# Convolution stage of a two-layer encoder: diagonals loaded, gate from PSUM, two staggered tap lanes, norm in token rows

## The reference

```
h = x @ w_in + b_in                      # 1024 -> 2048
a, gate = jnp.split(h, 2, axis=-1)
h = a * jax.nn.sigmoid(gate)
h = depthwise causal convolution of h, 31 taps per channel, + b_dw
h = jax.nn.silu(layer_norm(h, ln_g, ln_b))
mix = h @ w_out + b_out
x = layer_norm(DEEPNORM_ALPHA * x + mix, ln1_g, ln1_b)      # norm 0
```

## Time and profile before

| | value |
|---|---|
| median of three runs | 1872.43 us |
| the profiled execution's own time | 1870.53 us |
| its span | 1868.7 us |
| PE, DVE, ACT, POOL busy over the span | 97%, 69%, 50%, 15% |
| PE, DVE, ACT, POOL busy in 0 to 150 us | 128.7, 112.6, 93.0, 74.7 us |
| mean granted TensorE clock | 0.996 |
| bytes read from device memory | 316.95 MB |

### The profile page before, as it was taken

One profiled execution on the slowest core, in us unless ns is written; L12 is line 12 of the kernel. 1 busy time (PEld: TensorE's weight loads), 2 busy tenths in 40 slices (PEclk: granted clock), 3 DMA queues, 4 the chain that ended last, 5 costly groups with the idle time before them and its releaser, 6 DMA issues.

```text
span 1868.7 us, 31371 instructions
## 1 busy us (share of the span) xinstructions
PE 1816.6 (97%) x12212; PEld 1652.7 (88%) x12212; DVE 1285.7 (69%) x2400; ACT 926.7 (50%) x1593; POOL 272.5 (15%) x145
## 2 busy tenths in 40 slices
PE   7989999999999999999999999999999999999998
PEld 7669999999999888888777899999999988888886
DVE  5974893888965666666665559668888556666665
ACT  6754544544444544555534454445444454445553
POOL 7800746000000000000002228430000000000000
PEclk9999999999999999999999999999999999999999
DMA  7325555545556666667722356555555566666662
GB/s 251 113 71 164 153 161 169 157 159 159 158 171 205 193 194 195 195 203 255 258 93 68 117 154 182 169 159 158 159 159 159 181 204 194 194 195 193 214 216 100
DMA packets 87843, 320.05 MB, mean 171 GB/s; under 512 B 9872, under 2 KB 10384, under 8 KB 87568
## 3 DMA queue, kind: packets, MB, share of 16 engines
q1 hardware_dynamic: 84672, 307.42, 53.2%
q10 hardware_dynamic: 3024, 10.62, 1.6%
HBM read 316.95 MB, written 1.05 MB: 170 GB/s over the span
## 4 chain that ended last, share of the span: by engine, by line
PE 89%; DVE 6%; ACT 2%; DMA 1%; issue 1%; POOL 0%; SPq 0%; ACTq 0%; DVEq 0%
PE work L480 42%; PE y L528 38%; PE y L761 3%; PE y L508 2%; DVE y L1440 2%; PE work L636 1%; PE y L734 1%; DMA raw<-v 1%; DVE low L409 1%; PE y L583 1%; DMA raw<-mla_in 0%; ACT high L805 0%; DVE big L1252 0%; PE work L577 0%; DVE big L1423 0%
## 5 line engine op out<-in xcount | busy, mean ns | idle before, releaser
L805 ACT ACTIVATE high<-raw 128x1024 fp32r<-128x1024 f32 x473 | 497.8, 1054 | 476.8 <-PE work L480 430.3
L480 PE MATMUL work<-xT_high,high 128*128 128x256 f32 x2368 | 679.0, 287 | 14.8 <-POOL low L409 10.1
L480 PE MATMUL work<-xT_low,high 128*128 128x256 f32 x2368 | 671.3, 283 | 0.0
L480 PE MATMUL work<-xT_high,low 128*128 128x256 f32 x2368 | 671.1, 283 | 0.0
L409 DVE TENSOR_TENSOR low<-raw,high 128x1024 fp32r<-128x1024 f32 x384 | 469.4, 1224 | 249.2 <-ACT high L805 248.1
L480 PEld LDWEIGHTS work<-xT_high,high 128*128 128x128 f32 x2368 | 455.6, 192 | 17.3 <-POOL low L409 10.3
L480 PEld LDWEIGHTS work<-xT_low,high 128*128 128x128 f32 x2368 | 455.8, 192 | 0.0
L480 PEld LDWEIGHTS work<-xT_high,low 128*128 128x128 f32 x2368 | 455.4, 192 | 0.0
L409 POOL TENSOR_TENSOR low<-raw,high 128x1024 fp32r<-128x1024 f32 x89 | 220.8, 2489 | 249.9 <-ACT high L805 249.7
L1054 ACT ACTIVATE xT_high<-big 128x256 fp32r<-128x256 f32 x256 | 105.4, 416 | 285.3 <-PE y L528 285.1
L528 PE MATMUL y<-high,xT_high 128*128 128x512 f32 x696 | 216.9, 392 | 6.5 <-DVE xT_low L1468 5.2
(11 more groups left out here) (183 smaller groups left out, 1523.8 us busy)
## 6 DMA issues: line engine op xcount, KB each, us to landing
raw<-u SPq DMA_DIRECT2D x256, 512.0 KB, 3.5
raw<-v SPq DMA_DIRECT2D x256, 512.0 KB, 3.5
raw<-wq SPq DMA_DIRECT2D x32, 512.0 KB, 3.5
raw<-conv_in SPq DMA_DIRECT2D x16, 512.0 KB, 4.7
aux<-ln_par ACTq DMA_DIRECT2D x9, 512.0 KB, 5.8
raw<-conv_out SPq DMA_DIRECT2D x8, 512.0 KB, 3.6
raw<-mla_out SPq DMA_DIRECT2D x8, 512.0 KB, 3.7
raw<-mla_in SPq DMA_DIRECT2D x6, 512.0 KB, 4.5
```

Source lines behind the costliest of these rows:

```text
L480: mm = nc.tensor.matmul(out_, w[:, cols], m[:, k, :], start=(k == 0 and n == 0), stop=(k == KD - 1 and n == 2))
L805: A(high_at(c), raw[:, slot, :], ACT.Copy).then_inc(high_made, 1)
```

## The change

Part by part:

- **Start.** `x_cols` is loaded and split in four parts instead of two, and block 0 in two halves.
- **Gate.** ACT empties only the gate half. DVE's `glu` reads the value straight from PSUM with the bias (one instruction, PSUM and SBUF inputs). `conv_in` uses four banks instead of three.
- **Diagonals.** They come from device memory as a new input `diag` (4.06 MB, eight loads, issued by ACT beside blocks 4 to 12) instead of being made by ACT.
- **Taps of DVE.** Chunks 0 and 2 run in lane 0, chunks 1 and 3 in lane 1; lane 0 starts 12 taps ahead; chunk 4 is shared, 22 taps in lane 0 and 9 in lane 1, and one addition joins them. The later `glu`s stand between taps.
- **Norm.** PE transposes the chunks into token rows (in PSUM), some of them within the diagonals' matmuls. DVE takes BN statistics along rows, scales rows, PE transposes back group by group (two chunks of one token half), ACT applies SiLU in place in PSUM.
- **High and low of blocks 17 to 27.** POOL stops after block 16 and goes to the taps of chunk 7; afterwards it makes 18, 19, 21, 22, 25, 27, and DVE makes 17, 20, 23, 24, 26. ACT makes high 20 and 21 between the two halves' SiLU and high 22 to 27 after them. `scale_x(1)` and all four lows of 24 to 27 come ahead of norm 0.

```diff
@@ gpsimd
-            low_stage(0, FIRST["conv_out"] + 2 * RING)
+            pool.wait_ge(first_high, 1)
+            nc.gpsimd.tensor_tensor(low[:, 0, left], raw[:, 0, left], high[:, 0, left].bitcast(F32),
+                                    ALU.subtract).then_inc(first_low, 1)
...
+            low_stage(1, FIRST["conv_out"] + 1)
...
+            for c in OUT_LOWS_POOL:
+                make_low(pool, nc.gpsimd, c)
@@ tensor
+                elif name == "conv_in":
+                    out_ = work[:, c % BANKS, 0:T]
+                    if c >= BANKS:
+                        chunk, gate = divmod(c - BANKS, 2)
+                        pe.wait_ge(emptied if gate else glu_ok, chunk + 1)
...
             for c, k in enumerate(PE_CHUNKS):
                 pe.wait_ge(glu_ok, k + 1)
+                pe.wait_ge(diag_in[c], 16 * DIAG_LOADS)
                 for w in range(TAPS):
-                    pe.wait_ge(diag_ok, c * TAPS + w + 1)
...
+                    if c == 1 and w == ROWS_AT:
+                        pe.wait_ge(emptied, KD)
+                        pe.wait_ge(glu_ok, KD)
+                        pe.wait_ge(conv_done, SHARED)
+                        for n in range(SHARED):
+                            rows = to_rows(n)
+                        rows.then_inc(rows_mm, 1)
+                        pe.wait_ge(pe_conv_ok, 1)
+                        to_rows(PE_CHUNKS[0])
                 mm.then_inc(pe_conv, 1)
+            pe.wait_ge(conv_done, SHARED + 1)
+            to_rows(SHARED).then_inc(rows_mm, 1)
+            pe.wait_ge(pool_conv, 1)
+            to_rows(POOL_CHUNK)
+            pe.wait_ge(pe_conv_ok, 2)
+            to_rows(PE_CHUNKS[1]).then_inc(rows_mm, 1)
 
             def wait_conv(c):
+                n = c - FIRST["conv_out"]
                 wait_low(c)
-                wait_xT(PARTS + c - FIRST["conv_out"] + 1)
+                if n % PER_GROUP == 0:
+                    wait_xT(X_PARTS + n // PER_GROUP + 1)
+                if n == 2:
+                    to_columns(0, 1)
+                elif n in (4, 5):
+                    to_columns(1, n - 4)
+            to_columns(0, 0)
+            combine_tail(FIRST["conv_out"], 0, wait_conv, True, wait_conv_half)
@@ scalar
-                for n in range(DIAGONALS * t, DIAGONALS * (t + 1)):
-                    diagonal(n)
...
+            def silu(h, g):
+                act.wait_ge(cols_mm, GROUPS * h + g + 1)
+                for k in range(PER_GROUP * g, PER_GROUP * (g + 1)):
+                    chunk = group_bank(h, g)[:, k % PER_GROUP, :]
+                    ins = A(chunk, chunk, ACT.Silu,
...
+                A(xT_high[:, ks, h * P:(h + 1) * P], group_bank(h, g), ACT.Copy).then_inc(xT_hi_ok, 1)
+            for g in range(GROUPS):
+                silu(0, g)
+            make_high(rounded[0])
+            make_high(rounded[0])
+            for g in range(GROUPS):
+                silu(1, g)
             highs_to(FIRST["wq0"] + LEAD["wq0"] - 1)
@@ vector
             def glu(k):
-                dve.wait_ge(emptied, 2 * k + 2)
-                V.tensor_tensor(padded[:, k, PAD:PAD + T], value[:, k, :], value_gate[:, k, :],
-                                ALU.mult).then_inc(glu_ok, 1)
+                dve.wait_ge(emptied, k + 1)
+                V.scalar_tensor_tensor(padded[:, k, PAD:PAD + T], work[:, 2 * k % BANKS, 0:T],
+                                       conv_p[:, C_BIN + k:C_BIN + k + 1], value_gate[:, k, :],
+                                       ALU.add, ALU.mult).then_inc(glu_ok, 1)
...
+            for g in range(GROUPS):
+                conv_low(0, g)
+            make_low(dve, V, FIRST["conv_out"] + 4)
+            for g in range(GROUPS):
+                conv_low(1, g)
+            make_low(dve, V, FIRST["conv_out"] + 7)
...
             scale_x(0)
-            low_stage(FIRST["wq0"], FIRST["wq0"] + 2)
+            scale_x(1)
+            make_low(dve, V, FIRST["wq0"])
+            make_low(dve, V, FIRST["wq0"] + 2)
```

More of the change, by code:

```diff
@@ L533, in combine_block, with combine_second_half @@
                 return mm
-            def combine_second_half(part, norm, blocks, turn_after):
+            def combine_second_half(part, norm, blocks, turn_after, wait_block=None):
                 for n in blocks:
+                    if wait_block is not None:
+                        wait_block(n)
                     mm = part(n, (1,), (0,))
@@ L553, in combine_tail @@
                 mm.then_inc(y_half, 1)
-                combine_second_half(part, norm, range(TAIL), TURN_AFTER)
+                combine_second_half(part, norm, range(TAIL), TURN_AFTER, wait_half)
             def turn_half(n, h):
@@ L858, in _ @@
+            left, right = slice(0, D // 2), slice(D // 2, D)
+            round_x(0)
+            act.wait_ge(first_landed, 16)
+            A(high[:, 0, left], raw[:, 0, left], ACT.Copy).then_inc(first_high, 1)
+            round_x(1)
+            act.wait_ge(landed[0], 16)
+            A(high[:, 0, right], raw[:, 0, right], ACT.Copy).then_inc(high_made, 1)
+            rounded[0] = 1
+            for part in range(2, X_PARTS):
+                round_x(part)
+            highs_to(RING - 1)
             act.wait_ge(conv_par_in, 16)
@@ L859, in _, with load_diagonals @@
             act.wait_ge(consts, 4)
-            def diagonal(n):
-                c, w = n // TAPS, n % TAPS
-                at = C_TAPS + PE_CHUNKS[c] * TAPS + w
-                A(diagonals[:, c, w, :], ident[:], ACT.Identity,
-                  scale=conv_p[:, at:at + 1]).then_inc(diag_ok, 1)
+            def load_diagonals(n):
+                c, part = divmod(n, DIAG_LOADS)
+                edges = [(part + i) * TAPS // DIAG_LOADS * P for i in range(2)]
+                act.dma_start(diagonals[:, c, edges[0]:edges[1]],
+                              diag[:, c, edges[0]:edges[1]]).then_inc(diag_in[c], 16)
@@ new lines, in _ @@
+            glu(0)
+            for _ in range(AHEAD):
+                next_tap(0)
+                dve.wait_ge(v_step, count[0])
+            glu(1)
+            while done[0] < lengths[0] or done[1] < lengths[1]:
+                for lane in (1, 0):
+                    if done[lane] < lengths[lane]:
+                        next_tap(lane)
+                    else:
+                        dve.wait_ge(v_step, count[0])
+            dve.wait_ge(v_step, count[0])
+            V.tensor_tensor(conv[:, SHARED, :], conv[:, SHARED, :], total_of(0, 2),
+                            ALU.add).then_inc(conv_done, 1)
@@ new lines, in measure_rows @@
+            def measure_rows(h, g):
+                col = 24 * h + 6 * g
+                return V.bn_stats(row_stats[:, col:col + 6], row_group(h, g))
+            dve.wait_ge(x_in, 16 * HALVES)
+            dve.wait_ge(ln_in[0], 16 * LN_ROWS[0])
+            for g in range(GROUPS):
+                if g != 1:
+                    dve.wait_ge(rows_mm, max(g, 1))
+                for h in range(HALVES):
+                    last = measure_rows(h, g)
+                if g == 1:
+                    make_low(dve, V, FIRST["conv_out"] + 1)
@@ L1472, in _ @@
-            dve.wait_ge(x_in, 16 * HALVES)
-            dve.wait_ge(ln_in[0], 16 * LN_ROWS[0])
+            step(V.reciprocal(row_stats[:, 56:58], row_stats[:, 54:56]))
+            for h in range(HALVES):
+                for g in (0, 2, 3):
+                    rows, n = (work[:, 2 * h, :], PART) if g == 0 else (row_group(h, g), PER_GROUP)
+                    cols = slice(PER_GROUP * g * P, (PER_GROUP * g + n) * P)
+                    last = V.tensor_scalar(rows_n[:, h, cols], rows,
+                                           row_stats[:, 48 + 2 * h:49 + 2 * h], row_stats[:, 56 + h:57 + h],
+                                           ALU.subtract, ALU.mult)
+                    if g != 2:
+                        last.then_inc(norm_ok, 1)
```

285 lines of the change are left out of this document (152 added, 133 removed).

## The result

The changed kernel is slower: 1876.05 us, median of 20 runs (1869.32 to 1879.29), against 1871.18 us for the kernel before, timed beside it (20 runs, 1869.39 to 1874.66). The ratio is 1.0022, 95% interval 1.0014 to 1.0030. The forecast was 3.5 us less; it came out 4.9 us more. The profiled execution took 1875.27 us (span 1873.5) against 1870.53, so it shows the difference nearly whole.

The account below looks back on a forecast made before the run. PE was taken as the bound from the leading query blocks on, so E's change counts one for one: 133.73 to 130.2, hence 1872.43 - 3.5 = 1868.9 us; own range 1867 to 1871, wider range 1862.5 to 1873.5.

Parts of the forecast that it names:

- E: End of the first layer's conv_out, where PE starts the leading query blocks: 130.2 us, 3.5 less than 133.73.
- late chain: Behind conv_out's start, later blocks' highs and lows pass ACT, POOL and DVE late; norm 0 follows, PE waits 2.8 us.
- S: Time at which the token rows are complete ahead of the norm: 86.9 us, ended by PE, not DVE.
- Start: First conv_in blocks: block 0 begins near 7 instead of 9.86, block 1 at 13.25 instead of about 15.0.
- s: Delay of conv_in blocks by the diagonals' 4.06 MB of loads: 1.0 us, bounds 0 and 4.
- Rival 3: Diagonals' loads starve the weight ring; s could be 8 and goes into E in full: 1875.9 us, chance 0.11.
- Taps of DVE: DVE's first tap after glu 0 at 16.7, twelve alone at 0.52, the rest at 0.392: end 83.2 instead of 95.0.
- Additions of POOL: Chunk 7's taps: products start at 60, 29 additions at 0.694 and a last one, ending at 82.2.
- Low 17: DVE makes this conv_out block's low within the 3.7 us it has to spare before the rows are complete.
- Norm: From complete rows to conv_out: statistics to reciprocal 1.9 us, six scalings 3.1, low half 0.4; conv_out starts at 92.3.
- The turn: PE at norm 0 after conv_out's first halves: wait 2.8 us, transposes 0.8, last six right blocks 4.1.
- Load of block 26: Weight load that waits for low 23 ahead of norm 0: 3.6 us, landing at 115.9.

Follow-up runs that it names:

- e12: Changed kernel with only DVE's queue ahead of norm 0 shortened (x scaled earlier, low 26 and high 27 after the first half's norm); 1871.73 us, ratio 1.0002.
- e5: Changed kernel with the old start: input in two parts, block 0 of conv_in whole, diagonals still loaded; 1873.64 us, ratio 1.0013.
- e1: Changed kernel loading two diagonals in place of 62 and using them for every tap, so taps of chunks 5 and 6 are not computed; 1878.26 us.
- e2: Changed kernel with the diagonals made by ACT again, three per block, without their loads; 1877.37 us, ratio 1.0027.
- e6: Changed kernel with both the divided start and the diagonals' loads undone (ACT makes the diagonals); 1875.49 us, ratio 1.0024.
- e4: Changed kernel with the same diagonal bytes spread over more blocks, x and the norm's rows loaded behind them; 1875.77 us, ratio 1.0023.
- e10: e8 with a shorter DVE queue ahead of norm 0 (x scaled earlier, low 26 after the first half's norm); 1862.43 us, ratio 0.9952.
- e8: e6 with the lows of conv_out blocks 17 to 20 and highs of 19 to 21 made earlier; 1871.06 us, ratio 1.0001.
- e7: Kernel before with the divided start alone (input in four parts, block 0 in two halves); 1871.98 us, ratio 1.0006.
- e11: Changed kernel with both the early lows of conv_out and the shorter queue ahead of norm 0; 1861.43 us, ratio 0.9947.

## Why the prediction was wrong

The forecast was E = 130.2 for the leading blocks; 138.86 was measured. The late chain of the prediction held in its kind: PE waits for POOL's low 21 and 22 (0.20 and 4.14 us; also 1.60 for DVE's low 20, which it did not name), DVE for high 26, norm 0 is late, PE idles ahead of L617, the clock is at its lower level when `conv_out` starts (twelve matmuls in 5.31 us, forecast 5.1). It priced `conv_out` to E at 37.9 us, and 39.5 were measured. The step that failed is what stands ahead: S, the time at which the rows are complete, and the start of `conv_out`, forecast at 86.9 and 92.3, measured at 92.5 and 99.40. A gain of 16.4 us was expected there to pay for 13 behind, and there were 9.3. Of the 8.7 us by which E was missed, 7.1 lie ahead of `conv_out` and 1.6 behind its start. The items below are read from the one profile of the changed kernel. No run brought `conv_out` to before 97.36, and the same front in e12 was 2 us faster, so their sizes are good to some 2 us.

- **Start.** Block 1 at 14.24, forecast 13.25: its load, behind seven transfers, was issued at 4.03 and landed at 10.69 (chain, 6.64). In the kernel before it stands behind four and was issued at 2.63. "The bytes ahead of block 1 are the same" was true and not enough; there are three more issues ahead of it, 0.4 to 0.5 us each.
- **s.** Forecast 1.0. Fifteen blocks after 14.24 would have ended at 57.4; PE went on to the diagonals at 63.47, so s was 6.0; 1.6 of these are block 15 at the lower clock, which the term had not. In e12 the same front gives 61.08, in e5, with the bytes but the old start, 58.82. Rival 3 described this and gave 1875.9, next to the time measured. But e1, e2 and e6 took the bytes away, e4 spread them, and the time stayed. Its number was right by luck; its mechanism was not the loss. The waits of ACT for blocks (20.9 us, 12.5 in e12, 3.3 in the kernel before) say that the ring of three covered less than s = 1.0 assumed: the share of 0.91 of the earlier trace rows left little. The Trainium skill ("DMA: Bandwidth & Descriptors", "Issuing engines are not separate DMA queues"), by which the two streams take from the same 16 DMA engines, had been cited and not turned into a price.
- **Taps of DVE.** Forecast to end at 83.2; the last addition ended at 88.2. First tap 18.51 instead of 17.1 (1.4); twelve taps alone took 7.1 instead of 6.25, their pitch is 0.59, not 0.52 (0.85); two `glu`s waited 1.7 for late blocks; the rest took 1.0 more. The room between DVE's taps and the complete rows was there all the same (88.2 to 92.5), but only because PE was late too; in e5, with PE on time, it was 1.0 us (87.6 to 88.6).
- **Additions of POOL.** Forecast to end at 82.2; they ended at 89.5, since ACT's products began at 67.28 and not at 60, behind a block of `conv_out` that landed at 66.3. So POOL's first low behind them fell onto DVE's low 17 (in e5, where the additions end at 86.4, it was the second).
- **Low 17.** Priced inside the 3.7 us of room at its own 1.2. It took 3.40: POOL's low ran from 89.45 to 91.80, and DVE's ended 1.1 after it. In e5, with PE early, it took 3.19. What this costs is seen in e4 against e12: the rows are complete at 89.8 and 90.1 and the taps end at 88.7 and 88.4, but the low takes 3.39 in e4 and 1.21 in e12, and `conv_out` starts at 99.60 and 97.36. The prediction had the Trainium skill's rule on the port ("SBUF — State Buffer", "Who interferes with whom") and used it for low 23, where it came true (2.53), but not here. DVE's last statistics, behind low 17, begin at 92.81, just when the rows are complete at 92.5. These are two tracks of equal length. In e1, e2, e4 and e5 PE's is shorter (rows complete at 90.0, 89.2, 89.8 and 88.6), but DVE's isn't (last statistics at 93.5, 91.8, 93.3 and 92.0), and `conv_out` moved by 1.1 us at most.
- **Norm.** From the rows to `conv_out` 6.9 us, forecast 5.4; of that DVE's low has 0.4, and the statistics to the reciprocal took 2.7 instead of 1.9 (four pieces of 256 were left, not two).
- **The turn.** PE waited 2.95 (forecast 2.8), but the transposes took 1.97 (forecast 0.8), because the granted clock fell after the wait (0.72 from 130 to 134), and the six right blocks behind them 4.6 (forecast 4.1). The lower clock was reckoned at the start of `conv_out` and not here.
- **Load of block 26.** 4.94 us, forecast 3.6.
- **"Moving `scale_x(1)` and two lows ahead of norm 0 saves nothing."** Right, but the reverse should have been asked: what it costs. e12 puts it at 4.3 us while the lows of `conv_out` are late, and e10 against e8 at 8.6 once they are early.

The chance of slower, 0.12, was too small by the same error: the forecast's margin rested on 16.4 us ahead of `conv_out`, whose three tracks were summed with one value each, and each was late.

## What to carry to other kernels

When a stage in front gets shorter, look at what the old stage hid: here rounding work that lay beside the taps came to stand, in series over ACT, POOL and DVE, in front of the next norm, and it ate more than the stage gave. Before taking a suspect's share from one undone edit, look whether a second track ends at the same time, and how far two profiles of the same front differ; five edits to the start and the loads (e1, e2, e4 to e6) moved `conv_out` by 1.3 us at most, less than the 2.0 between two profiles of one front, and two edits at the place that PE really waited for gave 14.6 us. An engine's queue ahead of a norm that everyone waits for is to hold nothing that can be done in its idle time before or after.

## What the runs showed of the hardware

- A wait of PE of a few us between dense work was followed by a lower granted clock, a shorter one not: after 3.75 us of wait in e1 it was 0.50 for the next 4 us, and the same instructions took 7.75 us instead of 5.00; after 2.95 us in the changed kernel they took 6.38; after 1.72 us in e6 they took 5.05, at 1.00. e12, with no wait there, needed 4.97.
- A DVE subtraction with two SBUF inputs and one of POOL did not run side by side, and the one that started first had its own time. In e4 POOL's started at 89.94 and DVE's at 89.96: 2.34 and 3.39 us. In e12 DVE's started at 89.65 and POOL's at 89.72: 1.21 and 3.34 us. So a difference of under 0.1 us in the start decided over 2 us on DVE.
- DVE taps that each wait for the one before have a pitch of 0.59 us (11 in 6.41), two alternating lanes 0.39 to 0.40 (15 in 5.96, 14 in 5.57).
- The kernels with the divided start differ between each other in DVE's first tap by 2.8 us (18.51 to 21.26), though their programs are the same or nearly the same up to there (e12's is the same: 20.58); those with the old start by 0.4. Why the divided start is less steady stays open.
- Single profiles differ behind 150 us, where no edit reaches: e7's leading blocks start 2.0 us later than those of the kernel before (135.55 to 133.57) and its span is 1.4 us shorter (1867.3 to 1868.7); e8 and e6 start them 0.2 us apart (135.17, 135.34) and their spans are 3.3 apart (1867.8, 1871.1). Over all kernels the time from the first full query block to the end lies between 1718.0 (e7) and 1725.0 us (e11), 1721.4 in the kernel before and 1721.1 in the changed one. What causes these 7 us stays open; an effect of that size is to be read from the medians.
